# Other places in SBUF for the four slots of split weights in a two-layer trunk on TensorE

## The chip, the cores and the metric

The kernel runs on one core of a Trainium2 chip. The metric is the device time of one execution in microseconds (us). Three runs of the kernel before gave 2313.58, 2314.15 and 2316.32 us.

## The reference

The reference is a trunk of two residual layers on x of 256 positions by 2048 channels in float32. Only the shape of the work matters here:

```python
for l in range(2):
    u = x @ w_in[l]                       # 2048 x 6144 (6152 in layer 1)
    mix = branches(u) @ w_out[l]          # layer 0: convolution and HGRN2; layer 1: two attentions
    x = layer_norm(ALPHA * x + mix)
    h = square(relu(x @ mlp_w1[l])) @ mlp_w2[l]   # 2048 x 8192 and 8192 x 2048
    x = layer_norm(ALPHA * x + h)
```

All of the large weight matrices are read once from HBM, in float32, and multiplied with 256 rows of activations.

## The kernel before

A float32 product is made of three products in the type float32r. An operand is split into a high part (rounded to float32r) and a low part (the rest), and high x high, high x low and low x high are summed in PSUM.

The weights come in chunks of CK = 2 blocks of 128 x 512. A ring of RING = 4 slots holds them. For chunk s the sync engine loads `raw[:, s % 4]`, ScalarE copies it to `w_hi[:, s % 4]` (lines 440 and 647), and VectorE writes the rest, raw minus w_hi, to `w_lo[:, s % 4]` (lines 744 and 1084). Then TensorE makes the chunk's 12 products in `products` (lines 1210 to 1212): two halves of the rows, two blocks, three products each. The stationary operand is a 128 x 128 block of the activations (x_hi and x_lo, or c_hi and c_lo), the moving operand a 128 x 512 block of w_hi or w_lo. There are 768 chunks, so 9216 such products. Semaphores give the order: a slot is freed by `chunk_used`, the load waits for `lo_ready` of the chunk four before, TensorE for `lo_ready` of its own.

The feed-forward layers are loops written for every engine. In the mixer layers a hand-written order puts the small work behind chunks (`behind_even`, `behind_odd`): transposes at lines 1273, 1287 and 1563, the HGRN2 levels, the attention products (line 1448 makes one kind of scores, in plain float32 with 256 columns). One piece of it is of use here, `forget_logits`, whose products are 256 columns wide and in float32r; the stationary block moves by 8 columns for each k:

```python
for k in range(KT):
    cols = slice(k * HEADS, k * HEADS + P)
    pe.matmul(o_, wf_hi[:, cols], x_hi[:, k, :], start=(k == 0), stop=False)
    pe.matmul(o_, wf_hi[:, cols], x_lo[:, k, :], start=False, stop=False)
    ins = pe.matmul(o_, wf_lo[:, cols], x_hi[:, k, :], start=False, stop=(k == KT - 1))
```

How tensors lie in SBUF: they are allocated one behind the other. raw, w_hi, w_lo, x_hi, x_lo, c_hi and c_lo have 16,384 bytes in every partition each, a multiple of 256, so all of them begin at the same place within 256 bytes. A slot of w_hi or w_lo is 4096 bytes, a block of 512 columns 2048 bytes, a block of 128 activations 512 bytes. So in the kernel before every operand of lines 1210 to 1212, moving or stationary, begins at one and the same place within 256 bytes.

Of the kernel before, what the change touches and what calls it, by code (L numbers as in the profile page):

```python
# [20 lines left out]
F32, F32R, I8 = mybir.dt.float32, mybir.dt.float32r, mybir.dt.int8  # L21
ACT, ALU, AX = mybir.ActivationFunctionType, mybir.AluOpType, mybir.AxisListType
# [3 lines left out]
P = 128  # L26
RT = S // P
KT = D // P
N = 512
CK = 2  # L30
# [53 lines left out]
RING = 4  # L84
# [32 lines left out]
def trunk(nc, x, ev_w_in, ev_conv_w, ev_conv_b, ev_conv_ln_g, ev_conv_ln_b, hgrn_lb_logits, ev_gnorm_g, ev_w_out,  # L117
          od_w_in, fox_b_f, rel_bias, od_w_out, ln_mix_g, ln_mix_b, mlp_w1, mlp_w2, ln_mlp_g, ln_mlp_b, out):
    w_in, w_out = [ev_w_in[0], od_w_in[0]], [ev_w_out[0], od_w_out[0]]
    with ExitStack() as ctx:  # L120
        def sb(name, shape, dt):
            return ctx.enter_context(nc.sbuf_tensor(name, shape, dt))

        def sem(name):
            return ctx.enter_context(nc.semaphore(name))


        raw = sb("raw", [P, RING, CK, N], F32)
        w_hi = sb("w_hi", [P, RING, CK, N], F32R)
        w_lo = sb("w_lo", [P, RING, CK, N], F32R)  # L130
        x_hi = sb("x_hi", [P, KT, S], F32R)
        x_lo = sb("x_lo", [P, KT, S], F32R)
        c_hi = sb("c_hi", [P, KT, S], F32R)
# [83 lines left out]
        hi_ready, lo_ready = sem("hi_ready"), sem("lo_ready")  # L217
# [53 lines left out]
        def raw_wait(eng, s):  # L271

            eng.wait_ge(raw_full[s % RING], 16 * (s // RING + 1))
# [152 lines left out]
        def _(act):  # L426
            at = [0]
            n = [0]
# [6 lines left out]
            def split(s):  # L435
                raw_wait(act, s)
                if s >= RING:

                    act.wait_ge(chunk_used, s - RING + 1)
                act.activation(w_hi[:, s % RING], raw[:, s % RING], ACT.Copy).then_inc(hi_ready, 1)  # L440

            def upto(s):
                while at[0] <= s:
                    split(at[0])
                    at[0] += 1
# [132 lines left out]
            for s in range(38, SLOT_MLP[0]):  # L578
# [4 lines left out]
                for half, base in enumerate(LEVEL_SLOT):  # L583
                    k = s - base - 1
# [33 lines left out]
                if s == MEAN_SLOT + 9:  # L618
# [3 lines left out]
                    for c in range(8):  # L622
                        ins = act.activation(csq[:, c, :], cv[:, c, :], ACT.Silu, scale=cpar[:, 1, c:c + 1],
                                             bias=cpar[:, 2, c:c + 1])
# [13 lines left out]
            def mlp_tile(base, tbase, layer, b, i, last=False):  # L638

                first = base + i * CPT + RING  # L640
                for c in range(CPT):
                    s = first + c
                    if last and b * (2 * NT * CPT) + s >= SLOTS:
                        break
                    act.wait_ge(raw_full[s % RING], b * (16 * 2 * NT * CPT // RING) + 16 * (s // RING + 1))
                    act.wait_ge(chunk_used, b * (2 * NT * CPT) + (s - RING + 1))
                    act.activation(w_hi[:, s % RING], raw[:, s % RING], ACT.Copy).then_inc(hi_ready, 1)  # L647
                    if c == 1 and 1 <= i <= NT:
                        act.wait_ge(pair_full[0], b * NT + (USE[0]["h", layer, 0] + i))
                        act.activation(c_hi[:, 4 * (i - 1):4 * i, :], quad[0], ACT.Copy).then_inc(h_hi, 1)  # L650
                if i < NT:

                    t = tbase + i
                    act.wait_ge(chunk_used, b * (2 * NT * CPT) + (base + (i + 1) * CPT))
                    act.activation(urow[i % 2], gemm[t % 2][:, :, :], ACT.Relu).then_inc(relu_done, 1)
                    act.wait_ge(relu_done, b * NT + (layer * FB * NT + i + 1))
                    act.activation(urow[i % 2], urow[i % 2], ACT.Square).then_inc(h_row, 1)
# [21 lines left out]
            for g in range(4):  # L679
# [23 lines left out]
                for q in range(RT):  # L703
                    width = (q + 1) * P
                    v = sm[:, q * HG * P:q * HG * P + HG * width].rearrange("p (h k) -> p h k", h=HG)
                    for h in range(HG):
                        i = q * HG + h
                        ins = act.activation(v[:, h, :], v[:, h, :], ACT.Exp, bias=mx[:, i:i + 1],
                                             accum_out=sums[:, i:i + 1])
# [15 lines left out]
        def _(dve):  # L725
            at = [0]
            n = [0]

            def mark(ins):

                n[0] += 1
                ins.then_inc(dve_link, 1)
                return n[0]
# [4 lines left out]
            def split(s):  # L738

                dve.wait_ge(hi_ready, s + 1)  # L740
                raw_wait(dve, s)
                if s >= RING:
                    dve.wait_ge(chunk_used, s - RING + 1)
                dve.tensor_tensor(w_lo[:, s % RING], raw[:, s % RING], w_hi[:, s % RING].bitcast(F32), ALU.subtract  # L744
                                  ).then_inc(lo_ready, 1)

            def upto(s):
                while at[0] <= s:
                    add_before(at[0])
                    split(at[0])  # L750
                    at[0] += 1
# [112 lines left out]
            k = mark(dve.tensor_tensor(lbl[:, 0, :], lbl[:, 0, :], lb, ALU.subtract))  # L864
# [191 lines left out]
            def add_block(layer, b, j, t, end, last):  # L1056

                for r, done in enumerate((x_sum0, x_sum)):
                    if r == 0:
                        dve.wait_ge(rows_done, b * (2 * NT) + (t + 1))  # L1060
                    else:
                        dve.wait_ge(chunk_used, b * (2 * NT * CPT) + end)
                    Xj = X[:, r, j * N:(j + 1) * N]
                    dve.scalar_tensor_tensor(out=Xj, in0=Xj, scalar=factor[:, bass.ds(b, 1)], in1=gemm[t % 2][:, r, :],  # L1064
                                             op0=ALU.mult, op1=ALU.add).then_inc(done, 1)
                    dve.wait_ge(done, b * NT + (x_sums[0] + j + 1))
                    tile_stats(j, r)
                if last and j == NT - 1:
                    statistics((1 + FB) * NT * (layer + 1), 2 * layer + 2)

            def mlp_tile(layer, b, i, last=False):
                base, tbase = SLOT_MLP[layer], TILE_MLP[layer]
                first = base + i * CPT + RING
                for c in range(CPT):
                    s = first + c
                    if c == CPT - 1 and i >= NT:

                        add_block(layer, b, i - NT, tbase + i, base + (i + 1) * CPT, last)
                    if last and b * (2 * NT * CPT) + s >= SLOTS:
                        continue  # L1080
                    dve.wait_ge(hi_ready, b * (2 * NT * CPT) + (s + 1))
                    dve.wait_ge(raw_full[s % RING], b * (16 * 2 * NT * CPT // RING) + 16 * (s // RING + 1))
                    dve.wait_ge(chunk_used, b * (2 * NT * CPT) + (s - RING + 1))
                    dve.tensor_tensor(w_lo[:, s % RING], raw[:, s % RING], w_hi[:, s % RING].bitcast(F32), ALU.subtract  # L1084
                                      ).then_inc(lo_ready, 1)
                    if c == 1 and 1 <= i <= NT:
                        dve.wait_ge(h_hi, b * NT + (layer * NT * FB + i))
                        dve.tensor_tensor(c_lo[:, 4 * (i - 1):4 * i, :], quad[0],  # L1088
                                          c_hi[:, 4 * (i - 1):4 * i, :].bitcast(F32), ALU.subtract
                                          ).then_inc(h_ready, 1)  # L1090
# [112 lines left out]
        def _(pe):  # L1203
            def products(acc, hi, lo, k, slot, first, last):

                for r in range(RT):
                    rows = slice(r * P, (r + 1) * P)
                    for c in range(CK):
                        begin, end = first and c == 0, last and c == CK - 1
                        pe.matmul(acc[:, r, :], hi[:, k + c, rows], w_hi[:, slot, c, :], start=begin, stop=False)  # L1210
                        pe.matmul(acc[:, r, :], hi[:, k + c, rows], w_lo[:, slot, c, :], start=False, stop=False)  # L1211
                        ins = pe.matmul(acc[:, r, :], lo[:, k + c, rows], w_hi[:, slot, c, :], start=False, stop=end)  # L1212
                    if last and r == 0:
                        ins.then_inc(rows_done, 1)
                ins.then_inc(chunk_used, 1)

            def chunk(acc, act_, k, s, first, last):

                pe.wait_ge(lo_ready, s + 1)
                products(acc, act_[0], act_[1], k, s % RING, first, last)  # L1220
# [32 lines left out]
            def acquire(layer, i):  # L1253

                if i >= 2:
                    pe.wait_ge(*tile_out[layer][i - 2])
                elif layer:

                    pe.wait_ge(x_sum, (PARTS + FB) * NT - 1 + i)
                return gemm[(TILE0[layer] + i) % 2]  # L1260
# [245 lines left out]
            for layer in range(DEPTH):  # L1506
                behind = (behind_even, behind_odd)[layer]
                s0 = SLOT0[layer]
                for i in range(12):
                    s, t = at  # L1510
                    acc = acquire(layer, i)
# [6 lines left out]
                for part in (EVEN_OUT, ODD_OUT)[layer]:  # L1518
                    for j in range(NT):
                        s, t = at  # L1520
                        acc = acquire(layer, t - TILE0[layer])
# [73 lines left out]
```

## Time and profile before

| what | value |
|---|---|
| median of three runs | 2314.15 us (2313.58 to 2316.32) |
| span of the profiled execution | 2314.1 us |
| TensorE matmuls busy | 2251.9 us, 97% |
| weight loads into the array busy | 1868.4 us, 81% |
| VectorE busy | 1367.9 us, 59% |
| ScalarE busy | 1068.1 us, 46% |
| read from HBM | 414.79 MB, 180 GB/s |
| mean granted clock of TensorE | 0.988 |

The profiled execution has no time beside its span that differs from it; its span agrees with the median of the timed runs. "Busy" of TensorE is the union of the recorded matmuls, which overlap one another: a matmul's duration holds its way through the array as well, so the distance from one start to the next is what counts for the time.

### The profile page before, as it was taken

To read this page: it belongs to the slowest core of one execution; us is meant where nothing else is said; L and a number is where in the kernel's file an instruction comes from. 1 tells how busy PE (TensorE), PEld (TensorE's weight loads), DVE (VectorE), ACT (ScalarE), POOL (GpSimd) and SP (SyncE) were. 2 spreads that over 40 slices of the span, in tenths; PEclk is the share of its full clock that TensorE was granted. 3 is DMA by queue.
4 is the path that set the end of the run, shared out by engine and by line. 5 is a ranking of instruction groups with operands and counts; after the bars stand their busy time and mean duration, and the time that the engine had idled before them with its cause. 6 is when DMAs were issued, how large, how long until landed. Compare 5 with 4: busy or idle time off the path is not lost.

```text
span 2314.1 us, 28894 instructions
## 1 busy us (share of the span) xinstructions
PE 2251.9 (97%) x10331; PEld 1868.4 (81%) x10331; DVE 1367.9 (59%) x1489; ACT 1068.1 (46%) x1163; POOL 34.1 (1%) x64
## 2 busy tenths in 40 slices
PE   8999999799999999999989999998999999999997
PEld 7888788688888888888878888887888888888885
DVE  4898986745545545545565545567455455455455
ACT  4555564354344344344344444434444444443543
POOL 2000000100000000000000000000000000000000
PEclk9999999899999999999999999999999999999998
DMA  7555545665665665666645555565656666656653
GB/s 240 170 158 158 170 127 177 190 197 189 192 189 185 191 190 183 197 184 189 193 156 162 166 180 164 168 192 177 188 189 194 184 190 193 184 189 194 188 188 122
DMA packets 213546, 418.70 MB, mean 181 GB/s; under 512 B 12777, under 2 KB 13857, under 8 KB 212400
## 3 DMA queue, kind: packets, MB, share of 16 engines
q1 hardware_dynamic: 211616, 406.90, 57.5%
q0 software_dynamic: 1808, 10.04, 1.2%
q8 instruction: 93, 1.52, 0.3%
q14 instruction: 29, 0.24, 0.0%
HBM read 414.79 MB, written 2.10 MB: 180 GB/s over the span
## 4 chain that ended last, share of the span: by engine, by line
PE 61%; issue 32%; DVE 5%; ACT 1%; DMA 1%; POOL 0%; POOLq 0%; SPq 0%; DVEq 0%; ACTq 0%
PE gemm L1210 19%; PE gemm L1212 19%; PE gemm L1211 19%; DVE lnp L969 1%; DVE w_lo L744 1%; PE pair L1330 1%; DMA raw<-in_ev_w_out 1%; DVE X L817 1%; DVE X L816 1%; PE pair L1563 1%; PE pair L1273 1%; ACT w_hi L440 0%; PE pair L1287 0%; PE pair L1403 0%; PE pair L1475 0%
## 5 line engine op out<-in xcount | busy, mean ns | idle before, releaser
L1084 DVE TENSOR_TENSOR w_lo<-raw,w_hi 128x1024 fp32r<-128x1024 f32 x508 | 621.6, 1224 | 663.2 <-ACT w_hi L647 663.2
L647 ACT ACTIVATE w_hi<-raw 128x1024 fp32r<-128x1024 f32 x508 | 537.8, 1060 | 774.5 <-PE gemm L1212 774.5
L1210 PE MATMUL gemm<-w_hi,x_hi 128*128 128x512 f32 x1792 | 710.5, 397 | 5.5 <-DVE w_lo L744 4.0
L1212 PE MATMUL gemm<-w_hi,x_lo 128*128 128x512 f32 x1792 | 702.2, 392 | 0.0
L1211 PE MATMUL gemm<-w_lo,x_hi 128*128 128x512 f32 x1792 | 701.7, 392 | 0.0
L1210 PE MATMUL gemm<-w_hi,c_hi 128*128 128x512 f32 x1280 | 500.8, 391 | 4.2 <-DVE X L772 2.5
L1212 PE MATMUL gemm<-w_hi,c_lo 128*128 128x512 f32 x1280 | 498.7, 390 | 0.0
L1211 PE MATMUL gemm<-w_lo,c_hi 128*128 128x512 f32 x1280 | 498.6, 389 | 0.0
L744 DVE TENSOR_TENSOR w_lo<-raw,w_hi 128x1024 fp32r<-128x1024 f32 x260 | 316.4, 1222 | 208.9 <-ACT w_hi L440 208.6
L440 ACT ACTIVATE w_hi<-raw 128x1024 fp32r<-128x1024 f32 x260 | 272.7, 1056 | 304.2 <-PE gemm L1212 276.8
L1210 PEld LDWEIGHTS gemm<-w_hi,x_hi 128*128 128x128 f32 x1792 | 339.2, 189 | 78.5 <-DVE w_lo L744 5.0
L1212 PEld LDWEIGHTS gemm<-w_hi,x_lo 128*128 128x128 f32 x1792 | 338.8, 189 | 71.8
L1211 PEld LDWEIGHTS gemm<-w_lo,x_hi 128*128 128x128 f32 x1792 | 339.4, 189 | 68.3
L1210 PEld LDWEIGHTS gemm<-w_hi,c_hi 128*128 128x128 f32 x1280 | 240.7, 188 | 54.6 <-DVE X L772 2.9
L1212 PEld LDWEIGHTS gemm<-w_hi,c_lo 128*128 128x128 f32 x1280 | 240.6, 188 | 50.2
L1211 PEld LDWEIGHTS gemm<-w_lo,c_hi 128*128 128x128 f32 x1280 | 240.8, 188 | 49.5
L969 DVE SCALAR_TENSOR_TENSOR lnp<-scr,lnp 128x256 f32<-128x256 f32 x240 | 100.3, 477 | 0.0
L788 DVE BATCH_NORM_STATS2 stats<-X 128x6 f32<-128x512 f32 x80 | 55.6, 695 | 2.7
L1287 PE MATMUL pair<-ident,X 128*128 128x128 f32 x128 | 22.3, 316 | 33.3 <-DVE X L828 23.0
L1064 DVE SCALAR_TENSOR_TENSOR X<-X,factor,gemm 128x512 f32<-128x512 f32 x64 | 47.1, 735 | 7.1 <-PE gemm L1212 7.1
L1287 PEld LDWEIGHTS pair<-ident,X 128*128 128x128 f32 x128 | 16.6, 161 | 39.3 <-issue 30.4
L1088 DVE TENSOR_TENSOR c_lo<-pair,c_hi 128x1024 fp32r<-128x1024 f32 x32 | 38.9, 1217 | 0.0
(195 smaller groups left out, 831.1 us busy)
## 6 DMA issues: line engine op xcount, KB each, us to landing
raw<-in_mlp_w SPq DMA_DIRECT2D x512, 512.0 KB, 3.9
raw<-in_ev_w_in SPq DMA_DIRECT2D x96, 512.0 KB, 3.7
raw<-in_od_w_in SPq DMA_DIRECT2D x96, 512.0 KB, 3.7
raw<-in_ev_w_out SPq DMA_DIRECT2D x32, 512.0 KB, 4.4
raw<-in_od_w_out SPq DMA_DIRECT2D x32, 512.0 KB, 4.4
lnp<-in_ln_mix_g POOLq DMA_DIRECT2D x2, 1024.0 KB, 5.9
lnp<-in_ln_mix_b POOLq DMA_DIRECT2D x2, 1024.0 KB, 9.2
lnp<-in_ln_mlp_g POOLq DMA_DIRECT2D x2, 1024.0 KB, 4.9
```

What stands on the lines that cost most here:

```text
L440: act.activation(w_hi[:, s % RING], raw[:, s % RING], ACT.Copy).then_inc(hi_ready, 1)
L647: act.activation(w_hi[:, s % RING], raw[:, s % RING], ACT.Copy).then_inc(hi_ready, 1)
L744: dve.tensor_tensor(w_lo[:, s % RING], raw[:, s % RING], w_hi[:, s % RING].bitcast(F32), ALU.subtract).then_inc(lo_ready, 1)
L788: dve.bn_stats(stats[:, r, j, :], X[:, r, j * N:(j + 1) * N]).then_inc(stats_ready, 1)
L969: ins = dve.scalar_tensor_tensor(out=cv[:, ch, :], in0=src, scalar=cw[:, ch, j:j + 1], in1=cv[:, ch, :], op0=ALU.mult, op1=ALU.add)
L1064: dve.scalar_tensor_tensor(out=Xj, in0=Xj, scalar=factor[:, bass.ds(b, 1)], in1=gemm[t % 2][:, r, :], op0=ALU.mult, op1=ALU.add).then_inc( ...
L1084: dve.tensor_tensor(w_lo[:, s % RING], raw[:, s % RING], w_hi[:, s % RING].bitcast(F32), ALU.subtract).then_inc(lo_ready, 1)
L1088: dve.tensor_tensor(c_lo[:, 4 * (i - 1):4 * i, :], quad[0], c_hi[:, 4 * (i - 1):4 * i, :].bitcast(F32), ALU.subtract).then_inc(h_ready, 1)
L1210: pe.matmul(acc[:, r, :], hi[:, k + c, rows], w_hi[:, slot, c, :], start=begin, stop=False)
L1211: pe.matmul(acc[:, r, :], hi[:, k + c, rows], w_lo[:, slot, c, :], start=False, stop=False)
L1212: ins = pe.matmul(acc[:, r, :], lo[:, k + c, rows], w_hi[:, slot, c, :], start=False, stop=end)
L1287: ins = pe.transpose(quad[i % 2][:, c, r * P:(r + 1) * P], X[:, r, (k0 + c) * P:(k0 + c + 1) * P], ident[:, :])
```

## The change

Each of w_hi and w_lo becomes one flat buffer that is 64 elements (256 bytes) longer, and the four slots are views into it that begin 4, 8, 56 and 60 elements later than before. In bytes: slot 0 begins 16 further into 256 than the activations do, slot 1 32, slot 2 224 (which is 32 before the next multiple), slot 3 240 (16 before it). w_hi and w_lo have the same offset in the same slot. raw, the activations and everything else keep their place within 256 bytes. Order, waits, loads and the arithmetic are the same; the other lines of the diff only follow the new way to name a slot.

```diff
         raw = sb("raw", [P, RING, CK, N], F32)
-        w_hi = sb("w_hi", [P, RING, CK, N], F32R)
-        w_lo = sb("w_lo", [P, RING, CK, N], F32R)
+
+        def places(name):
+
+            t = sb(name, [P, RING * CK * N + 64], F32R)
+            begin = [q * CK * N + off for q, off in enumerate((4, 8, 56, 60))]
+            return [t[:, b:b + CK * N].rearrange("p (c n) -> p c n", c=CK) for b in begin]
+
+        w_hi, w_lo = places("w_hi"), places("w_lo")
...
-                act.activation(w_hi[:, s % RING], raw[:, s % RING], ACT.Copy).then_inc(hi_ready, 1)
+                act.activation(w_hi[s % RING], raw[:, s % RING], ACT.Copy).then_inc(hi_ready, 1)
...
-                dve.tensor_tensor(w_lo[:, s % RING], raw[:, s % RING], w_hi[:, s % RING].bitcast(F32), ALU.subtract
+                dve.tensor_tensor(w_lo[s % RING], raw[:, s % RING], w_hi[s % RING].bitcast(F32), ALU.subtract
                                   ).then_inc(lo_ready, 1)
...
-                        pe.matmul(acc[:, r, :], hi[:, k + c, rows], w_hi[:, slot, c, :], start=begin, stop=False)
-                        pe.matmul(acc[:, r, :], hi[:, k + c, rows], w_lo[:, slot, c, :], start=False, stop=False)
-                        ins = pe.matmul(acc[:, r, :], lo[:, k + c, rows], w_hi[:, slot, c, :], start=False, stop=end)
+                        pe.matmul(acc[:, r, :], hi[:, k + c, rows], w_hi[slot][:, c, :], start=begin, stop=False)
+                        pe.matmul(acc[:, r, :], hi[:, k + c, rows], w_lo[slot][:, c, :], start=False, stop=False)
+                        ins = pe.matmul(acc[:, r, :], lo[:, k + c, rows], w_hi[slot][:, c, :], start=False, stop=end)
```

## Rows read from the trace of the kernel before

**Rows 1.** The page's head: span, and busy time of each engine.
```profile
span 2314.1 us, 28894 instructions
PE 2251.9 (97%) x10331; PEld 1868.4 (81%) x10331; DVE 1367.9 (59%) x1489; ACT 1068.1 (46%) x1163; POOL 34.1 (1%) x64
```
**Rows 2.** The page's groups: line, engine, tiles, shapes, count | busy us, mean ns | idle before.
```profile
L1084 DVE TENSOR_TENSOR w_lo<-raw,w_hi 128x1024 fp32r<-128x1024 f32 x508 | 621.6, 1224 | 663.2 <-ACT w_hi L647 663.2
L647 ACT ACTIVATE w_hi<-raw 128x1024 fp32r<-128x1024 f32 x508 | 537.8, 1060 | 774.5 <-PE gemm L1212 774.5
L1210 PE MATMUL gemm<-w_hi,x_hi 128*128 128x512 f32 x1792 | 710.5, 397 | 5.5 <-DVE w_lo L744 4.0
...
L1210 PE MATMUL gemm<-w_hi,c_hi 128*128 128x512 f32 x1280 | 500.8, 391 | 4.2 <-DVE X L772 2.5
...
L744 DVE TENSOR_TENSOR w_lo<-raw,w_hi 128x1024 fp32r<-128x1024 f32 x260 | 316.4, 1222 | 208.9 <-ACT w_hi L440 208.6
```
**Rows 3.** The page's chain that ended last, by engine.
```profile
PE 61%; issue 32%; DVE 5%; ACT 1%; DMA 1%; POOL 0%; POOLq 0%; SPq 0%; DVEq 0%; ACTq 0%
```
**Rows 4.** The longest waits of TensorE: us in total, times, longest us.
```profile
PE pair L1287 <- DVE X L828: 23.0, 6, 8.8
...
PE gemm L1210 <- DVE w_lo L744: 4.7, 3, 3.4
```
**Rows 5.** Timeline of TensorE, the start of one chunk and of the next: start us, length us.
```profile
999.80 0.39 PE L1210 MATMUL gemm<-w_hi,x_hi 128*128 128x512 f32 x1
1000.03 0.39 PE L1211 MATMUL gemm<-w_lo,x_hi 128*128 128x512 f32 x1
...
1002.52 0.39 PE L1210 MATMUL gemm<-w_hi,x_hi 128*128 128x512 f32 x1
```
**Rows 6.** Two windows inside the feed-forward layers; the sixth column is the granted clock.
```profile
903.00:980.00 77.00, 77.00 (x341) 63.77 (x340) 43.16 (x42) 29.72 (x28) 0.00 (x0) 1.00 0.62 192
1860.00:1940.00 80.00, 80.00 (x354) 66.24 (x353) 44.66 (x43) 31.19 (x30) 0.00 (x0) 1.00 0.63 192
```
**Rows 7.** Line 1210 in the window 903 to 983 us: duration ns minimum/median/maximum.
```profile
L1210 PE MATMUL gemm<-w_hi,c_hi x118: 389/389/389, 903.0 to 982.6; 128*128 128x512 f32 x118
L1210 PEld LDWEIGHTS gemm<-w_hi,c_hi x117: 187/188/188, 903.5 to 982.4; 128*128 128x128 f32 x117
```
**Rows 8.** Line 1212 before a pause, and the weight load that comes next.
```profile
L1212 PE MATMUL gemm<-w_hi,c_lo x1: 388/388/388, 431.2 to 431.2; 128*128 128x512 f32 x1
...
440.36 0.18 PEld L1287 LDWEIGHTS pair<-ident,X 128*128 128x128 f32 x1 [9.16 <-issue]
```
**Rows 9.** Line 1448, plain float32 products with 256 columns: duration ns.
```profile
L1448 PE MATMUL pair<-scr x32: 379/379/382, 1245.5 to 1470.4; 128*128 128x256 f32 x32
```
**Rows 10.** Timeline of TensorE while the granted clock is at half.
```profile
445.12 0.63 PE L1210 MATMUL gemm<-w_hi,x_hi 128*128 128x512 f32 x1
445.55 0.63 PE L1211 MATMUL gemm<-w_lo,x_hi 128*128 128x512 f32 x1
445.98 0.63 PE L1212 MATMUL gemm<-w_hi,x_lo 128*128 128x512 f32 x1
```
**Rows 11.** The forget-gate products: duration ns of the three lines; first k and ninth k.
```profile
L1418 PE MATMUL pair<-x_hi,wf_hi x16: 276/279/283, 1201.9 to 1207.2; 128*128 128x256 f32 x16
...
L1420 PE MATMUL pair<-x_hi,wf_lo x16: 278/280/283, 1202.1 to 1207.4; 128*128 128x256 f32 x16
...
1201.90 0.28 PE L1418 MATMUL pair<-x_hi,wf_hi 128*128 128x256 f32 x1
...
1204.72 0.28 PE L1418 MATMUL pair<-x_hi,wf_hi 128*128 128x256 f32 x1
```
**Rows 12.** The three lines behind a group of transposes, 655.3 to 657.0 us: duration ns.
```profile
L1210 PE MATMUL gemm<-w_hi,x_hi x3: 389/389/477, 655.1 to 656.6; 128*128 128x512 f32 x3
L1211 PE MATMUL gemm<-w_lo,x_hi x3: 389/393/395, 655.4 to 656.8; 128*128 128x512 f32 x3
L1212 PE MATMUL gemm<-w_hi,x_lo x3: 389/393/398, 655.6 to 657.0; 128*128 128x512 f32 x3
```
**Rows 13.** The first product behind the forget-gate products, and the timeline after it.
```profile
L1210 PE MATMUL gemm<-w_hi,x_hi x1: 394/394/394, 1207.5 to 1207.5; 128*128 128x512 f32 x1
...
1207.77 0.39 PE L1211 MATMUL gemm<-w_lo,x_hi 128*128 128x512 f32 x1
1207.99 0.39 PE L1212 MATMUL gemm<-w_hi,x_lo 128*128 128x512 f32 x1
```

More of the change, by code:

```diff
@@ L646, in mlp_tile @@
                     act.wait_ge(chunk_used, b * (2 * NT * CPT) + (s - RING + 1))
-                    act.activation(w_hi[:, s % RING], raw[:, s % RING], ACT.Copy).then_inc(hi_ready, 1)
+                    act.activation(w_hi[s % RING], raw[:, s % RING], ACT.Copy).then_inc(hi_ready, 1)
                     if c == 1 and 1 <= i <= NT:
@@ L1083, in mlp_tile @@
                     dve.wait_ge(chunk_used, b * (2 * NT * CPT) + (s - RING + 1))
-                    dve.tensor_tensor(w_lo[:, s % RING], raw[:, s % RING], w_hi[:, s % RING].bitcast(F32), ALU.subtract
+                    dve.tensor_tensor(w_lo[s % RING], raw[:, s % RING], w_hi[s % RING].bitcast(F32), ALU.subtract
                                       ).then_inc(lo_ready, 1)
```

## The prediction

> **What bounds the kernel now.** I read the page from the top. The profiled span is 2314.1 us, the same as the median of the three timed runs (2314.15, from 2313.58 to 2316.32), so the sum below is made against that figure without a correction. TensorE is busy for 97% of it and no other engine passes 59% [rows 1]. The groups show what it is busy with: 3 x 1792 + 3 x 1280 = 9216 products of 128 x 512 at lines 1210 to 1212, almost without idle time before them [rows 2]. The chain that ended last is laid on the same three lines, with little of VectorE, ScalarE or the loads in it [rows 3]. The list of waits agrees: what TensorE waited for in total is some tens of microseconds, at the layer norms and at the start, and one wait for w_lo of 4.7 us in all [rows 4].
>
> So what matters is how far apart the products start. In the timeline of a quiet stretch twelve products, one chunk, take 1002.52 - 999.80 = 2.72 us, or 226.7 ns each [rows 5]. 9216 of them make 2089 us, nine tenths of the span. One nanosecond for each product is 9.2 us, 0.4% of the time. An edit that only shifts where operands lie can act through this number or not at all.
>
> **What the 226.7 ns consist of.** The granted clock is 1.00 in the quiet windows [rows 6], which is the 2.4 GHz level, and there 512 columns at one column a cycle are 213.3 ns. The rest is 13 ns. Three readings tell where it can come from.
>
> First, the duration column stands about 162 ns above the start-to-start distance (389 against 226.7), so it can be used as a finer ruler for one product. In the quiet window all 118 of line 1210 last 389 ns, minimum and maximum alike [rows 7]. They have an activation block being loaded beside them each time.
>
> Second, the product of line 1212 at 431.2 us is the last one before a pause. The next load of a stationary block starts at 440.36 us, so nothing is loaded while it runs, and it lasts 388 ns [rows 8]. That is the fact I lean on most. If the load of the next stationary block cost the running product anything in the steady state, this one should have been some 10 ns shorter. It isn't, so in the present layout there is next to nothing to be regained from the pair "moving operand and stationary operand".
>
> Third, plain fp32 products with 256 columns, which occupy the array for about as long (216 ns apart if the same 162 to 163 ns are taken off 379), last 379 ns [rows 9]. At the lower clock level, 1.2 GHz, the fp32r products start 427 ns apart (445.12, 445.55, 445.98), which is 512 columns at 1.2 GHz and nothing on top [rows 10]. So the 10 ns above the fp32 case belong to fp32r read at full speed, and I take them as the moving stream's own.
>
> **Does the place of an operand matter at all?** The trace has one experiment on it already. The forget-gate products at lines 1418 to 1420 use stationary blocks of wf_hi and wf_lo that move on by 8 columns, 32 bytes, for each k, so that they come round after eight k, 256 bytes. All moving operands there keep one place. Their durations are not equal: 276 to 283 ns, median 279 or 280, while their neighbours with fixed places repeat to the nanosecond [rows 7, 11]. The starts say that the pattern repeats: eight k take from 1201.90 to 1204.72 us, 2.82 us, 117.5 ns a product, where 256/512 of the quiet distance would be 113.3. So a changing relative place goes with about 4 ns more for each product than the quiet pattern would give, spread over +-3.5 ns, and the shortest one (276 - 162 = 114) is at the quiet rate and not below it.
>
> A rule speaks to this. The Trainium skill, page "TensorE: Matmul & The Clock Gate", section "Step-by-step: what each phase is for", says that TensorE has two independent SBUF read ports and that loading the next weights takes no read bandwidth from the running matmul. The trace agrees in the present layout [rows 8]; the spread at the forget-gate products does not agree [rows 11]. By the rule the change is worth nothing and the time stays at 2314; that is a rival below.
>
> **The other memory of the stream.** After an interruption the stream does not go back to 389 ns at once. Behind the transposes at 655.08 us the products last 393, 398, 389, 395 and 393 ns, and only then 389 for good (the three lines' minima, medians and maxima in this window; the first product, 477, still contains the load before it) [rows 12]. That is 4 + 9 + 0 + 6 + 4 = 23 ns lost in a run of five, with the same operands' places as in the quiet stretch. Behind the forget-gate products, where no pause lies but the places of the operands change, the first one lasts 394 and the run ends there: 5 ns [rows 13]. I read this as a rhythm that the stream has to find again after a change, and 389 as the length inside it. Nothing in the disturbed runs that I sum lasts less than 389.
>
> **The change part by part.** No instruction is added, removed or moved, and no wait.
>
> The splits (508 at line 1084 and 260 at line 744, 768 chunks) write to and read from places 16 to 240 bytes further on. VectorE takes 1.22 us and ScalarE 1.06 us for one [rows 2], together 2.3 us of a chunk's 2.72 us, with four slots in the ring and the wait of ScalarE on a freed slot as the releaser. Even 0.1 us more each would stay inside. I cost this at nothing. Without that cover the 0.1 us would be paid 768 times, but the four slots give about three chunks of cover. The loads into raw are untouched.
>
> The buffers grow by 64 elements, 256 bytes, so that every later tensor keeps its place within 256. Nothing there.
>
> The moving operands now change their place by slot: for every chunk of 12 products the place differs from the one before it, by +16, -64 (32 to 224), +16 and +32 bytes. In the kernel before there is one relative place for everything. This is the only term. For each of the 768 chunk changes its bounds are 0 (no memory of the place) and 23 ns (each change is as bad as an interruption) [rows 12]. The row that is nearest to it is the 5 ns behind the forget-gate products [rows 13], a change of place without a pause. I take 5 ns for the two small moves of 16 bytes and 23 ns for the two larger ones: (2 x 5 + 2 x 23)/4 = 14 ns, times 768 = 10.8 us. The sum is 2314.1 + 10.8 = 2324.9 us. All at 5 ns: 2318. All at 23 ns: 2331.8.
>
> **The rivals.**
> A, the time doesn't change. The stream only cares for its own steady rate, and the rhythm carries over from slot to slot. For it speaks that blocks 512 bytes and more apart (both row halves, both chunks c) all give 389 now, and the 388 of [rows 8]. Against it, the spread in [rows 11]. Time 2314.
>
> B, the rhythm is never found while the place is not the common one: each product costs what the five of the disturbed run cost on the mean, 393.6 - 389 = 4.6 ns. For it speaks the forget-gate pattern, which never became quiet in 48 products and lost about 4 ns in each. 9216 x 4.6 = 42 us, so 2356.5.
>
> C, the other sign. Equal places of moving and stationary operand are themselves what costs, and a small distance frees it. In [rows 11] the shortest product is 4 ns below the median. If the new places give half of that, 9216 x 2 = 18 us come off: 2296. If the whole 389 - 379 = 10 ns were such a cost [rows 7, 9], 92 us would come off: 2222. Against it stands the 388 of the product with no load beside it. It decides if a product in the quiet stretch lasts less than 388.
>
> **How the numbers follow.** A change under 0.2% (4.6 us) can't be told from none in this kernel. Forecast (loss at the chunk changes): 0.36. Rival A: 0.27. Rival B: 0.15. Rival C: 0.22, of which 0.05 for the large form. The forecast's lower end of 5 ns per change is 3.8 us and would count as the same, for which I move 0.05. So faster 0.22, same 0.32, slower 0.46. The range reaches from the small form of C to B: 2296 to 2357, which leaves out about 0.05 to 0.1 below and 0.05 above.
>
> **What would show it.** Right: in a quiet stretch the durations at lines 1210 to 1212 are no longer 389 alone; after each change of slot come a few at 393 to 398 and then 389; twelve products take up to 2.74 us in place of 2.72. B: they never come back to 389. A: all at 389 as before. C: durations below 388, and a chunk shorter than 2.72 us. The lengths of the splits at lines 647 and 1084 should stay at 1.06 and 1.22 us, and TensorE's waits for w_lo at a few microseconds. What would make the forecast wrong most easily is that the 388 of the product before a pause doesn't mean what I take it to mean, since the ends of matmuls are modelled in this profile.

## The result, and the profile after

The changed kernel takes 2363.85 us (2360.58 to 2367.05, four runs) against 2315.24 us for the kernel before beside it: a ratio of 1.0204, 95% interval 1.0189 to 1.0219. It is 48.6 us slower. The forecast was 2325 us, slower by 10.8 us; the time lies above the range of 2296 to 2357.

The page's groups of the changed kernel (its lines behind the allocation are six higher: 1210 is now 1216, 1084 is 1090, 647 is 653):

```profile
L1090 DVE TENSOR_TENSOR w_lo<-raw,w_hi 128x1024 fp32r<-128x1024 f32 x508 | 621.8, 1225 | 697.1 <-ACT w_hi L653 697.1
L653 ACT ACTIVATE w_hi<-raw 128x1024 fp32r<-128x1024 f32 x508 | 537.9, 1060 | 808.8 <-PE gemm L1218 808.8
L1216 PE MATMUL gemm<-w_hi,x_hi 128*128 128x512 f32 x1792 | 717.5, 400 | 3.8 <-DVE w_lo L750 3.2
...
L1216 PE MATMUL gemm<-w_hi,c_hi 128*128 128x512 f32 x1280 | 508.6, 397 | 3.3 <-DVE X L778 2.2
```

The splits are as long as before, 1225 and 1060 ns against 1224 and 1060 [rows 2]. The products are not: 400 and 397 ns on the mean where they were 397 and 391. Over all six groups the page's means go from 397, 392, 392, 391, 390 and 389 to 400, 396, 396, 397, 396 and 396 ns, weighted 4.8 ns more. 9216 x 4.8 = 44 us, nearly all of the 48.6. TensorE's longest waits and its wait for w_lo did not grow (against [rows 4]):

```profile
PE pair L1293 <- DVE X L834: 21.2, 6, 7.1
...
PE gemm L1216 <- DVE w_lo L750: 3.2, 3, 2.4
```

One line in a quiet window (minimum/median/maximum ns), and the timeline over 48 products, four chunks, one round of the ring:

```profile
L1216 PE MATMUL gemm<-w_hi,c_hi x72: 390/394/398, 930.3 to 979.9; 128*128 128x512 f32 x72
```
```profile
940.03 0.40 PE L1216 MATMUL gemm<-w_hi,c_hi 128*128 128x512 f32 x1
...
951.21 0.40 PE L1216 MATMUL gemm<-w_hi,c_hi 128*128 128x512 f32 x1
```

There is no 389 for good any more [rows 7]; the lengths run from 390 to 398 in the middle of a feed-forward layer, and at this line a load takes the 187 to 189 ns that it took. A round takes 11.18 us where four chunks took 4 x 2.72 = 10.88 [rows 5], that is 6.2 ns more for each product. The page's 4.8 is smaller for two reasons: the page's means also hold the stretches at the lower clock and around interruptions, where less changed, and the recorded lengths grew less than the way between starts (394.5 ns on the mean here, 5.5 above 389). The granted clock is 1.00 here as it was [rows 6]:

```profile
903.00:980.00 77.00, 77.00 (x337) 62.24 (x336) 41.19 (x39) 31.87 (x31) 0.00 (x0) 1.00 0.59 185
```

The lengths have an order that the line hides: each slot has a pattern of its own. Line 1217 in four chunks that follow one another, slots 0 to 3 (16, 32, 224 and 240 bytes):

```profile
L1217 PE MATMUL gemm<-w_lo,c_hi x4: 390/394/398, 945.2 to 947.3; 128*128 128x512 f32 x4
L1217 PE MATMUL gemm<-w_lo,c_hi x4: 393/395/397, 948.0 to 950.0; 128*128 128x512 f32 x4
L1217 PE MATMUL gemm<-w_lo,c_hi x4: 395/396/396, 950.7 to 952.8; 128*128 128x512 f32 x4
L1217 PE MATMUL gemm<-w_lo,c_hi x4: 394/394/394, 953.5 to 955.6; 128*128 128x512 f32 x4
```

The last thing to look at is the product before a pause, on which the prediction leaned. At the pause of [rows 8] it now lasts 390 ns, at another one 398. The next load starts at 818.45 us there, so again nothing is loaded beside it:

```profile
L1218 PE MATMUL gemm<-w_hi,c_lo x1: 390/390/390, 437.4 to 437.4; 128*128 128x512 f32 x1
L1218 PE MATMUL gemm<-w_hi,c_lo x1: 398/398/398, 817.8 to 817.8; 128*128 128x512 f32 x1
...
818.45 0.19 PEld L1216 LDWEIGHTS gemm<-w_hi,x_hi 128*128 128x128 f32 x1 [0.66 <-DVE w_lo L1090]
```

Fourteen such products without a load beside them stand in this trace, and they last from 387 to 402 ns; the twelve of the kernel before last 388 each. So the length of such a product follows the state in which the stream has come to it. It doesn't show what a load costs. That takes the ground from under the prediction's main argument.

### The profile page after: what moved, and what is told of

The parts are those of the page before. It is cut to its first block, busy times and chain, and to the rows that moved or that the text cites. A ratio compares the mean times of both kernels' runs of the same rounds, so it can differ in the third digit from the quotient of the medians.

```text
span 2361.3 us, 28894 instructions
## 1 busy us (share of the span) xinstructions
PE 2301.5 (97%) x10331; PEld 1868.1 (79%) x10331; DVE 1368.5 (58%) x1489; ACT 1068.6 (45%) x1163; POOL 34.4 (1%) x64
## 4 chain that ended last, share of the span: by engine, by line
PE 57%; issue 33%; DVE 7%; ACT 1%; DMA 1%; POOL 0%; POOLq 0%; DVEq 0%; SPq 0%; ACTq 0%
PE gemm L1216 18%; PE gemm L1218 18%; PE gemm L1217 18%; DVE lnp L975 3%; DVE w_lo L750 1%; PE pair L1336 1%; DVE X L823 1%; DMA raw<-in_ev_w_out 1%; DVE X L822 1%; PE pair L1569 1%; ACT w_hi L446 1%; PE pair L1279 0%; PE pair L1409 0%; PE pair L1293 0%; PE pair L1481 0%
## 5 line engine op out<-in xcount | busy, mean ns | idle before, releaser
L1090 DVE TENSOR_TENSOR w_lo<-raw,w_hi 128x1024 fp32r<-128x1024 f32 x508 | 621.8, 1225 | 697.1 <-ACT w_hi L653 697.1
L653 ACT ACTIVATE w_hi<-raw 128x1024 fp32r<-128x1024 f32 x508 | 537.9, 1060 | 808.8 <-PE gemm L1218 808.8
L1217 PE MATMUL gemm<-w_lo,x_hi 128*128 128x512 f32 x1792 | 709.1, 396 | 0.0
L1216 PE MATMUL gemm<-w_hi,c_hi 128*128 128x512 f32 x1280 | 508.6, 397 | 3.3 <-DVE X L778 2.2
L1218 PE MATMUL gemm<-w_hi,c_lo 128*128 128x512 f32 x1280 | 507.1, 396 | 0.0
L1217 PE MATMUL gemm<-w_lo,c_hi 128*128 128x512 f32 x1280 | 506.7, 396 | 0.0
```

What stands on the lines that cost most here:

```text
L653: act.activation(w_hi[s % RING], raw[:, s % RING], ACT.Copy).then_inc(hi_ready, 1)
L1090: dve.tensor_tensor(w_lo[s % RING], raw[:, s % RING], w_hi[s % RING].bitcast(F32), ALU.subtract).then_inc(lo_ready, 1)
L1216: pe.matmul(acc[:, r, :], hi[:, k + c, rows], w_hi[slot][:, c, :], start=begin, stop=False)
L1217: pe.matmul(acc[:, r, :], hi[:, k + c, rows], w_lo[slot][:, c, :], start=False, stop=False)
L1218: ins = pe.matmul(acc[:, r, :], lo[:, k + c, rows], w_hi[slot][:, c, :], start=False, stop=end)
```

## The experiments

"Distance" is the place of the moving operand (w_hi, w_lo) within 256 bytes less that of the stationary one (the activations). Ratios are against the kernel before on the same chip. Lengths are from the window 930 to 980 us, in the middle of a feed-forward layer, where nothing else is said. The recorded length of a product is the way from its start to the next product's start and some 162 ns more (159 to 165 with only the low activations moved), product by product. A long one can therefore be a slow product or a late start of the next.

**First: is it the change between slots, the distance, or the moving operand's own place?** The expectations call these three theory S (the change between slots, the prediction's), theory R (the distance) and theory M (the moving operand's own place). The changed kernel with one offset for all slots:

```diff
-            begin = [q * CK * N + off for q, off in enumerate((4, 8, 56, 60))]
+            begin = [q * CK * N + off for q, off in enumerate((8, 8, 8, 8))]
```

> All four slots of w_hi and w_lo begin 32 bytes further into 256 than the activations; no move from slot to slot. Theory S (the stream loses its rhythm only where the place changes from one slot to the next): back to 2315 us, durations of 389 ns in quiet stretches. Theory R (the distance between moving and stationary operand sets the length) and theory M (the place of the moving operand alone sets it): slower, about as slot 1 of the changed kernel, whose products last 395 ns on the mean, so 9216 x 6 ns = 55 us more, 2370 us, or less if a fixed distance lets the stream settle.

Measured: 2368.91 us, ratio 1.0229 (1.0212 to 1.0246). No place changes from slot to slot and the loss is larger than in the changed kernel. S is out as the main cause.

```profile
L1216 PE MATMUL gemm<-w_hi,c_hi x72: 393/395/397, 930.3 to 980.0; 128*128 128x512 f32 x72
```

In order of time its products last 393, 396, 394, 397 ns and so on, over and over. Where a pause cuts this off, the product before it lasts 388, 392 or 397 ns, always the same after the same five, in all 15 cases. That is the state told of above.

The next kernels start from the kernel before, or from this one with another offset. Both operands 32 bytes further:

```diff
+        pad_w = sb("pad_w", [P, 8], F32)
         w_hi = sb("w_hi", [P, RING, CK, N], F32R)
...
         c_lo = sb("c_lo", [P, KT, S], F32R)
+        pad_c = sb("pad_c", [P, 56], F32)
```

> w_hi, w_lo and all activations begin 32 bytes further into 256 than before, so the distance between moving and stationary operand is 0 and only their common place is new. Theory R: 2315 us and 389 ns. Theory M: slow, as the kernel with all four slots at 32 bytes and the activations where they were. Theory S: 2315 us.

Measured: 2315.67 us, ratio 0.9999 (0.9990 to 1.0009), and 389 ns throughout. The common place doesn't matter for this step of 32 bytes. Nor does the distance between raw and the split weights, which is 32 bytes here as in the run before.

Only the activations 32 bytes further (the first pad stands before x_hi):

```diff
         w_lo = sb("w_lo", [P, RING, CK, N], F32R)
+        pad_x = sb("pad_x", [P, 8], F32)
         x_hi = sb("x_hi", [P, KT, S], F32R)
```

> The split weights stay, the activations (and what lies behind them up to the pad) begin 32 bytes further into 256: the distance is 32 bytes with the other sign, the moving operand is where it was. Theory M: 2315 us and 389 ns. Theory R: slower by some 40 to 55 us. Theory S: 2315 us.

Measured: 2369.43 us, ratio 1.0227 (1.0210 to 1.0244), although no moving operand has moved. M is out too. What is left is R, the distance, and at 32 bytes both signs cost 54 us.

All slots 64 bytes further, `enumerate((16, 16, 16, 16))`:

> All four slots 64 bytes further than the activations. Theory S: 2315 us. Theories R and M with a period of 64 bytes: 2315 us; with the period of 256 bytes that the forget-gate products showed: another time, from 2300 to 2370 us.

Measured: 2333.01 us, ratio 1.0078 (1.0061 to 1.0095). The stream settles here, into a pattern over three products, one of which is even a nanosecond shorter than 389:

```profile
L1216 PE MATMUL gemm<-w_hi,c_hi x73: 394/394/394, 929.9 to 979.4; 128*128 128x512 f32 x73
L1217 PE MATMUL gemm<-w_lo,c_hi x73: 388/388/388, 930.2 to 979.6; 128*128 128x512 f32 x73
L1218 PE MATMUL gemm<-w_hi,c_lo x74: 392/392/392, 929.7 to 979.8; 128*128 128x512 f32 x74
```

**Second: through which pair does the distance work?** Each product has two stationary blocks near it, its own (loaded while the product before it ran) and the next one's (loaded while it runs itself). Only x_lo and c_lo 32 bytes further:

```diff
         x_hi = sb("x_hi", [P, KT, S], F32R)
+        pad_a = sb("pad_a", [P, 8], F32)
         x_lo = sb("x_lo", [P, KT, S], F32R)
+        pad_b = sb("pad_b", [P, 56], F32)
         c_hi = sb("c_hi", [P, KT, S], F32R)
+        pad_c = sb("pad_c", [P, 8], F32)
         c_lo = sb("c_lo", [P, KT, S], F32R)
+        pad_d = sb("pad_d", [P, 56], F32)
```

> Only x_lo and c_lo begin 32 bytes further; they are the stationary operand of the third product of each triple, and their block is loaded while the second product runs. If a load slows the product that runs beside it (theory N, next load), the second product of each triple gets longer than 389 ns and the other two do not, and the time rises by a third of the 54 us of the kernel with all slots at 32 bytes, to about 2333 us. If a product suffers from the distance to its own stationary block (theory O, own load), the third one gets longer, with the same time. If every product is longer, what counts is a rhythm over all of them.

Measured: 2367.70 us, ratio 1.0226 (1.0209 to 1.0243). In order of issue:

```profile
L1214 PE MATMUL gemm<-w_hi,c_hi x72: 394/396/396, 930.3 to 980.0; 128*128 128x512 f32 x72
L1215 PE MATMUL gemm<-w_lo,c_hi x72: 399/401/401, 929.8 to 979.5; 128*128 128x512 f32 x72
L1216 PE MATMUL gemm<-w_hi,c_lo x72: 388/390/390, 930.1 to 979.8; 128*128 128x512 f32 x72
```

The second product, beside which the moved block is loaded, gains 12 ns. The third, which works with the moved block, gains 1. By itself that looks like the load beside the product. But the first one gains 7 ns too, with nothing moved near it, and the time rises by 52 us, as much as with all slots moved, and not by a third of that. Neither pair theory foresaw that. Nor can the 401 be given to one pair: it may as well be a late start of the third product, and at 64 bytes, where all three products have the same distances, they last 394, 388 and 392 ns. Where no load stands beside the third product, before a pause, it is recorded with 397 or 398 ns in 12 of 13 cases, longer and not shorter than with one.

w_lo moved as well, so that each product and the load beside it have distance 0 (here no pad follows c_lo, so the tensors behind it lie 32 bytes further too):

```diff
         w_hi = sb("w_hi", [P, RING, CK, N], F32R)
+        pad_a = sb("pad_a", [P, 8], F32)
         w_lo = sb("w_lo", [P, RING, CK, N], F32R)
+        pad_b = sb("pad_b", [P, 56], F32)
         x_hi = sb("x_hi", [P, KT, S], F32R)
+        pad_c = sb("pad_c", [P, 8], F32)
         x_lo = sb("x_lo", [P, KT, S], F32R)
+        pad_d = sb("pad_d", [P, 56], F32)
         c_hi = sb("c_hi", [P, KT, S], F32R)
+        pad_e = sb("pad_e", [P, 8], F32)
         c_lo = sb("c_lo", [P, KT, S], F32R)
```

> w_lo and x_lo, c_lo begin 32 bytes further, w_hi and x_hi, c_hi where they were. Each product then has distance 0 to the block that is loaded beside it (w_hi beside x_hi twice, w_lo beside x_lo once per triple), while two of three products have a distance of 32 bytes to their own stationary block. Theory N (the load beside the product counts): back to 2315 us and 389 ns. Theory O (the own block counts) or the plain view that all operands must share one place: 2350 to 2370 us, as with the low activations alone (2368).

Measured: 2351.98 us, ratio 1.0161 (1.0144 to 1.0178), in a fixed pattern of 393, 397 and 391 ns:

```profile
L1216 PE MATMUL gemm<-w_lo,c_hi x73: 397/397/397, 930.0 to 980.0; 128*128 128x512 f32 x73
```

So the load beside the product is not what decides, or not alone. And w_lo alone, the first two pads:

> Only w_lo begins 32 bytes further. The second product of each triple then has a distance of 32 bytes to the load beside it (x_lo) and to its own block (x_hi). By the load beside the product alone, this is the low activations' case: 2368 us, with about +11 ns on the second product. If a change of the moving operand's place from one product to the next costs by itself, as the 38 us of the matched pairs may mean, both add: over 2380 us. If that change of place is harmless and the own block is what costs, about 2350 us.

Measured: 2365.65 us, ratio 1.0211 (1.0194 to 1.0228), with 395, 400 and 393 ns. It is the low activations' case again (396, 401, 390); the changes of the moving operand's place inside the triple did not add to it. Once more the longest product is the second. It has the distance to the load beside it and to its own block, so this run doesn't part the two.

**Third: is the 13 ns above 213 the load's?** In the two kernels of this part, some of the work is left out: all products except the first and the last of an accumulation make only 32 of their 128 output rows, so that their stationary block has 32 columns.

```diff
+                    few = slice(r * P, r * P + 32)
...
-                        pe.matmul(acc[:, r, :], hi[:, k + c, rows], w_lo[:, slot, c, :], start=False, stop=False)
+                        pe.matmul(acc[0:32, r, :], hi[:, k + c, few], w_lo[:, slot, c, :], start=False, stop=False)
```

> Layout of the kernel before. All products but the one that begins and the one that ends an accumulation have a stationary block of 32 columns instead of 128 (only 32 rows of the output are made by them, so most of the result is left out), so that the load beside a product is a quarter as long; moving operands, order and waits stay. If the 13 ns above 213 ns belong to the moving stream alone, as the prediction took it, durations stay about 389 ns less what a shorter block takes to drain, and starts 226.7 ns apart. If the load beside the product makes them, starts come nearer, toward 216 ns.

Measured: 2354.02 us in one run (before: 2315.67), so slower. The loads did get shorter, 108 ns where a full block takes 188 [rows 7], and the products longer:

```profile
L1212 PE MATMUL gemm<-w_lo,c_hi x73: 391/393/397, 929.6 to 979.6; 128*32 128x512 f32 x73
```
```profile
L1212 PEld LDWEIGHTS gemm<-w_lo,c_hi x72: 107/108/112, 930.1 to 979.4; 128*32 128x32 f32 x72
```

The same with all slots 32 bytes further:

> The same short stationary blocks with all four slots 32 bytes further. If the loads are what the distance works through, the difference between this and the kernel with short blocks and distance 0 shrinks from 54 us to a quarter or less. If it is the moving stream's place in some other way, it stays near 54 us.

Measured: 2340.88 us in one run, 13 us less than at distance 0. With short loads the sign of the distance's effect has turned, in one run each; the kernel before spreads over 3.4 us beside them. So the 13 ns don't come down with the load, which fits the prediction. But it also held the loads to be of no account, and a shorter load made the products longer. Distance 0 is shown to be the good one only with the loads of this kernel.

**Fourth: the map of distances, for all slots alike.** `enumerate` with 4, 24, 32, 48, 60, 64 and 1 elements, in this order.

> All four slots 16 bytes further. If the loss comes from the distance itself and the changes of place between slots add nothing, the changed kernel (16, 32, 224, 240; 2364 us) is about the mean of this one and the 2369 us of 32 bytes, so this one takes about 2359 us. If the changes from slot to slot are the larger part, as the prediction had it, this one comes out near 2315 to 2330 us.

Measured: 2355.92 us, ratio 1.0180 (1.0163 to 1.0197). It is near the 2359 that was expected of a distance without changes between slots. The last runs below suggest that a distance is not all that this one has.

> All four slots 96 bytes further. The forget-gate products were shortest near distances of 64 to 128 bytes. If distance 0 is the only one at which each product starts in the same phase, this is slower than 2320 us, as 32, 64 and 128 bytes were; if the forget-gate pattern carries over, it is the place to find a gain, 2300 us or less.

Measured: 2368.55 us, ratio 1.0238 (1.0220 to 1.0255). The forget-gate pattern doesn't carry over. Here too the three products of a triple last different times with the same distances, 392, 394 and 399 ns:

```profile
L1218 PE MATMUL gemm<-w_hi,c_lo x72: 399/399/399, 930.1 to 979.8; 128*128 128x512 f32 x72
```

> All four slots 128 bytes further than the activations, half of 256. With a period of 128 bytes the time is that of distance 0, 2315 us. With a period of 256 bytes it is another one; after +54 us at 32 and +18 us at 64 bytes, a fall with the distance says about 2315 us or a little less, while a distance of 0 as the only good one says 2325 to 2370 us.

Measured: 2360.16 us, ratio 1.0192 (1.0175 to 1.0209). The period is not 128 bytes.

> All four slots 192 bytes further, 64 before the next multiple. If only the size of the distance counts, 2333 us as at +64 bytes; at 32 bytes both signs gave 2369. If the sign counts at 64 bytes, another time between 2315 and 2370.

Measured: 2370.65 us, ratio 1.0244 (1.0227 to 1.0261), against 2333 at +64. At 64 bytes the sign counts.

> All four slots 240 bytes further, 16 before the next multiple of 256. If the changed kernel is the mean of its four distances (16: 2356, 32: 2369, 224: 2369 by the activations at 32, 240: this one), this one takes 4 x 2364 - 2356 - 2369 - 2369 = 2362 us. If changes from slot to slot add the prediction's 11 us, it is about 44 us less, 2318.

Measured: 2387.41 us, ratio 1.0308 (1.0291 to 1.0325). Both expectations miss. The mean ratio of the four distances (1.0180, 1.0229, 1.0227 and 1.0308) is 1.0236, the changed kernel has 1.0204. Its four different slots are thus some 7 us better than the four distances alone (224 bytes is taken from the kernel with the activations at 32).

The traces show where these 7 us are. Product by product over the whole trace, pauses left out, slots 0 to 3 of the changed kernel start their products 231.8, 233.3, 233.3 and 232.3 ns apart on the mean; the kernels with one of these distances alone have 231.7, 233.3, 233.3 and 235.2. Three slots run as their distance does alone, the fourth 2.9 ns faster, and 2304 x 2.9 = 6.7 us. In the changed kernel slot 3 runs mostly at 394 ns (the fourth line of the patterns above). The kernel with all slots at 240 bytes knows that pattern too, and another one; an interruption switches between them:

```profile
L1217 PE MATMUL gemm<-w_lo,x_hi x20: 394/394/394, 906.3 to 919.6; 128*128 128x512 f32 x20
...
L1217 PE MATMUL gemm<-w_lo,c_hi x71: 398/398/403, 929.6 to 979.3; 128*128 128x512 f32 x71
```

So one distance can have more than one steady length, and what came before picks it. Coming from slot 2, the stream enters the better one.

> All four slots 256 bytes further, a distance of 0 within 256, with the changed kernel's buffers and way to name a slot. If the place within 256 is all that counts: 2315 us and 389 ns. If the buffers or the views cost something of their own: slower.

Measured: 2316.20 us, ratio 1.0002 (0.9993 to 1.0012). The buffers of the split weights and the views cost nothing, and 256 bytes is as good as 0:

```profile
L1216 PE MATMUL gemm<-w_hi,c_hi x74: 389/389/389, 929.7 to 979.3; 128*128 128x512 f32 x74
```

> All four slots 4 bytes further, one element. If whole 16-byte lines are what meets: 2315 us, or slower only by what one more line per block costs (9216 x about 1 ns, under 10 us). If any distance breaks the common phase: about 2350 to 2370 us, as 16 bytes did.

Measured: 2401.75 us, ratio 1.0369 (1.0352 to 1.0387), the largest loss so far. To see if that is a distance at all, the weights and all activations together were put 4 bytes further, each group in one flat buffer:

```diff
+        W = RING * CK * N
+        ww = sb("ww", [P, 2 * W + 64], F32R)
+        w_hi, w_lo = (ww[:, 1 + i * W:1 + (i + 1) * W].rearrange("p (q c n) -> p q c n", q=RING, c=CK) for i in range(2))
+        xx = sb("xx", [P, 4 * KT * S + 64], F32R)
+        x_hi, x_lo, c_hi, c_lo = (xx[:, 1 + i * KT * S:1 + (i + 1) * KT * S].rearrange("p (k s) -> p k s", k=KT)
+                                  for i in range(4))
```

> w_hi, w_lo and all activations begin 4 bytes further, distance 0. If the distance is all that counts: 2315 us and 389 ns. If operands off a multiple of 16 bytes cost by themselves: slower, up to the 2402 us of the kernel in which only the weights are 4 bytes further.

Measured: 2407.75 us, ratio 1.0397 (1.0380 to 1.0415), with distance 0:

```profile
L1210 PE MATMUL gemm<-ww,xx x70: 400/401/475, 929.8 to 979.9; 128*128 128x512 f32 x70
L1211 PE MATMUL gemm<-ww,xx x69: 392/400/401, 930.1 to 979.4; 128*128 128x512 f32 x69
```

So a loss doesn't need a distance. The last run has both 16 bytes further, the same buffers with 4 elements in place of 1.

> w_hi, w_lo and all activations begin 16 bytes further, distance 0, in the same flat buffers as the kernel with 4 bytes. If lines of 16 bytes are what the 4 bytes broke: 2315 us and 389 ns. If the stream wants multiples of 32 bytes, or if the flat buffers cost something: slower, up to 2408 us.

Measured: 2364.08 us, ratio 1.0204 (1.0187 to 1.0221), again with distance 0, and the stream has settled, but at 396 ns instead of 389:

```profile
L1210 PE MATMUL gemm<-ww,xx x72: 396/396/396, 930.2 to 979.9; 128*128 128x512 f32 x72
L1211 PE MATMUL gemm<-ww,xx x72: 396/396/396, 929.7 to 979.4; 128*128 128x512 f32 x72
```

These two kernels have the same buffers and distance 0, and differ by 44 us, so the common place counts below 32 bytes. What 16 bytes cost against 0 is less sure: the flat buffer of the activations can't be told apart from the place, since no run has it at 32 bytes; the flat weights at 256 bytes were free. If the buffer is free too, then, with the 2315.67 us of both at 32 bytes, operands cost by themselves when they begin off a multiple of 32, counted from their place in the kernel before. The runs at 16 and 240 bytes, and slots 0 and 3 of the changed kernel, would then pay for two things at once, while 32, 64, 96, 128, 192 and 224 bytes are pure distances.

The Trainium skill, page "SBUF — State Buffer", section "Specifications (TRN2)", gives SBUF lines of 16 bytes, with a penalty for each crossing to a new line. An estimate from that: a block of 2048 bytes that begins 4 bytes into a line touches 129 lines instead of 128. The runs agree in the direction at 4 bytes. At 16 bytes a block touches no more such lines than before and its product still lasts 7 ns longer (396 against 389), so that rule is not enough.

## Why the prediction was wrong

**What bounds the kernel** held. The loss is in the products of lines 1210 to 1212: of the 47.2 us by which the profiled span grew, 46.1 lie between the start of one of them and the next start on TensorE. And the price of a nanosecond for each (9.2 us) is what turned 4.8 ns into 44 us.

**The cost of the splits, the loads and the longer buffers at nothing** held: 1225 and 1060 ns, and 1.0002 with all slots at 256 bytes.

**The failed step** is the sum's one term, "This is the only term", the price for a change of place from chunk to chunk: 14 ns times 768, 10.8 us. It puts the distance itself, held for a whole chunk, at nothing. That is what costs (and, for the slots at 16 and 240 bytes, perhaps also the start off a multiple of 32). One fixed distance of 32 bytes costs 54 us with no change between slots, all slots at 16 bytes cost 42 us, and the mixture costs about 7 us less than its parts. The changes between slots do act, but with the other sign: some -7 us in place of +10.8, all of it in slot 3.

**How it came to that** is the reading of [rows 8]. The 388 ns without a load beside it were taken to say that the load is of no account in the steady state. In the changed kernel such products last 387 to 402 ns, and in the kernel with only the low activations moved they are recorded some 8 ns longer than the same products with a load. The Trainium skill, page "TensorE: Matmul & The Clock Gate", section "Step-by-step: what each phase is for", which the prediction weighed, says that loading the next block takes no read bandwidth from the running product. By that alone the distance to the stationary block should not have mattered; moving the activations alone cost 54 us, the measurement decides, and rival A falls with it. A row that pointed the right way was there: the forget-gate products [rows 11], whose places change against each other with every k, never settled and cost about 4 ns more than the quiet pattern. The prediction gave rival B, which rests on it, 0.15, and leaned on one product before a pause.

**Rival B's size** was nearly right, 4.6 ns and 42 us, so 2356.5, against 4.8 ns and 48.6 us in all. That was in good part luck. It priced a stream that stays in the disturbed run of [rows 12]; what came instead is settled patterns, one for each slot, and 6.2 ns for each product in a quiet stretch. At 64 bytes the stream settles too, into 394, 388 and 392 ns, and loses only 18 us.

**That nothing is to be gained** (against rival C) held for each of the seventeen layouts tried with full products; the best are those with distance 0 on a multiple of 32 bytes, at 2315 and 2316 us. The reason given, that the 13 ns are the moving stream's own, is not shown. With loads of 108 ns the products did not get shorter, which fits it; they got longer, which says that the load has a hand in their length. No run here had a stream of products without loads.

**What stays open**: why a distance costs, why a common place 4 bytes further does, and whether one 16 bytes further does by itself. The 401 ns of the second product, when only the low activations are moved, point at the load beside it, but they don't show it: equal distances also give unequal lengths within a triple (392, 394 and 399 at 96 bytes), the first product gains 6 to 7 ns with no distance to anything near it, and the matched pairs still lost 38 us. The load beside a product, its own block and the state that its neighbours hand on were not separated.

## What to carry to other kernels

Where TensorE runs back to back on fp32r operands, give every operand of the stream, moving and stationary, the same place within 256 bytes, on a multiple of 32 (only 0 and 32 bytes were tried as that common place), and check it by the duration column in a quiet stretch. Here 389 ns, equal in minimum, median and maximum, was the mark of the good layout; 396 three times was as settled and cost 2%, so compare the length as well. Other places lost 1 to 4% here, and on the page it shows in the products' mean length and hardly anywhere else. And a product next to a pause is no test of what its neighbours cost, since it inherits the stream's state. Look at more than one stretch, too: one layout can run in different patterns between interruptions.

## What the runs showed of the hardware that was not expected

The loss by distance is gone again at 256 bytes and has no simple shape between: 2315 us at 0, 2369 at 32, 2333 at 64, 2369 at 96, 2360 at 128, 2371 at 192. It shows at the 2.4 GHz level only. At 1.2 GHz the starts were 0.43 us apart before the change [rows 10], and they are in the changed kernel:

```profile
449.15 0.63 PE L1218 MATMUL gemm<-w_hi,x_lo 128*128 128x512 f32 x1
449.57 0.63 PE L1216 MATMUL gemm<-w_hi,x_hi 128*128 128x512 f32 x1
450.00 0.63 PE L1217 MATMUL gemm<-w_lo,x_hi 128*128 128x512 f32 x1
```

The stream has a memory. The way back after an interruption [rows 12] goes over five products, and at 240 bytes a whole stretch runs in the pattern that the stream fell into at its start (394 ns, or 398 to 403).

Rounds of 48 products take fixed times. In the kernel with all slots at 32 bytes:

```profile
940.07 0.39 PE L1216 MATMUL gemm<-w_hi,c_hi 128*128 128x512 f32 x1
...
951.27 0.39 PE L1216 MATMUL gemm<-w_hi,c_hi 128*128 128x512 f32 x1
```

That is 11.20 us, 233.3 ns a product; the kernel with only the low activations moved has 951.06 - 939.86 = 11.20 us too, through quite other lengths, and the kernel before 10.88, 226.7 ns a product. The two differ by 6.7 ns, which is 16 cycles at 2.4 GHz. Seven kernels have these 11.20 us: all slots at 32, 96 and 192 bytes, the activations at 32, the low activations at 32, w_lo at 32, and both at 16. So one moved block in three could cost as much as all of them. Steps of the same 6.7 ns stand between three products of the settled patterns: 1167 ns for three of 389, then 394 + 388 + 392 = 1174 at 64 bytes, 393 + 397 + 391 = 1181 for the matched pairs, and 396 + 401 + 390 = 1187 with the low activations moved. From start to start that is 680.0, 686.7, 693.4 and 700.0 ns. Why these steps, and why a layout falls on one of them, no run here shows.
